# A decoder trunk: the first norm's shift and scale rows on TensorE, and layer 0's last mixer rows loaded with the gate weights

## The chip, the cores and the metric

The kernel runs on one core of a Trainium2 chip. A core has TensorE (matmuls, fp32 here), VectorE, ScalarE, GpSimd (POOL) and SyncE (SP), each with its own instruction stream; they meet only through semaphores. SP's stream issues nearly all weight DMAs. The metric is the device time of one execution in microseconds (us); lower is better.

## The reference, cut to what matters

Two layers run over 256 tokens of 1024 channels. Each has a SwiGLU FFN, a token mixer (an RWKV-7 branch beside an mLSTM branch, joined by sigmoid gates) and a second FFN. Before each part the hidden state is normed and modulated by rows that come from a vector `c`:

```
cond = silu(c)                                   # 1024 values
mod  = cond @ ada_w[l] + ada_b[l]                # 9 rows of 1024: sh0 sc0 gt0 sh1 sc1 gt1 sh2 sc2 gt2
h = rms_norm(x, g0) * (1 + sc0) + sh0;  x += 0.5 * (1 + gt0) * swiglu(h)
h = rms_norm(x, g1) * (1 + sc1) + sh1;  x += (1 + gt1) * token_mixer(h)
h = rms_norm(x, g2) * (1 + sc2) + sh2;  x += 0.5 * (1 + gt2) * swiglu(h)
```

`ada_w[l]` is 1024 x 9216, 37.7 MB a layer, and is used once. `sh0` and `sc0` of layer 0 are needed before the first FFN; `sc2` of layer 0 (columns 7168 to 8191, "the third scale rows") only after its mixer.

## The kernel before

**The start.** `c` is turned into a column and `cond` made. The 2048 columns of `sh0` and `sc0` come in four blocks of 512 columns, each in two DMAs of 512 rows (1 MB): block 0 from POOL's queue into `ada_stage`, blocks 1 to 3 from SP's into `ada_first`, in the order block 2, half of the first FFN weights, block 1, block 3. Blocks 2 and 3 are the scales of channels 0 to 511 and 512 to 1023, blocks 0 and 1 the shifts. Block 0 and 1 are summed by VectorE (`ada_sums`: multiply by a column of `cond`, add, eight times; then a 32x32 block transpose and a reduction; then `ada_columns` on TensorE). Block 2, and three quarters of block 3, are row products on TensorE with one column of `cond` as the weights (`ada_row`); ScalarE copies the row, and TensorE turns it into columns (`row_columns`). `half_factors(0)` and `half_factors(1)` make the scale and shift of the channels of each half, the normed tiles `hT` 0 to 3 and 4 to 7 follow, and `first_halves` multiplies the first four tiles before the last four exist.

**The ring.** All other weights pass through a ring of 12 cells of 4 KB a partition. `ring_places` gives each use its cells and names the use that had them before; SP waits in `room` until TensorE has counted that one free (`slot_free`), and TensorE waits with `landed` for a load. SP issues in program order, so a load that waits holds back all that follow.

**The other rows.** 1024 columns at a time, in four units of 1 MB, are brought by POOL's queue and summed by VectorE in places between its FFN work (`ada_at`): six such blocks in the first FFN of layer 0, five in its second.

**The mixer.** Its weights come as ten projection blocks, then eight gate units `ct` = 0 to 7 (1 MB, three cells taken, two filled), then branch and output weights. A gate unit is loaded in eight pieces of 128 KB over three lanes: a lane holds one piece at a time, and the last piece waits for all three. Gate units 0 and 1 are read by VectorE and TensorE early (the pairs `gates 0` and `gates 1`). For units 2 to 7 TensorE has 96 gate steps, numbered 32 to 127, one matmul of 256 columns each, which `GATE_PLACES` spreads as filler over the chain of small dependent products of the RWKV branch: "num" has steps 32 to 36, "n" 37 to 44, "a" 45 to 52, "b" 53 to 60, "c" 61 to 68, and so on. Unit `ct` begins at step 16 `ct`, with a wait for its load; so unit 3 begins at step 48, the fourth step of place "a". Unit 3 is loaded into the cells of unit 0, unit 4 into those of unit 1, unit 5 into those of unit 2, unit 6 into those of unit 3.

Every matmul of 128 rows and columns in fp32 shows as two records in the trace, a transpose by `turn` as one.

## Time and profile before

| | us |
|---|---|
| median of 3 runs | 1403.44 (1399.76 to 1404.1) |
| the profiled execution's own time | 1401.57 |
| its span, first to last instruction | 1399.8 |
| TensorE busy in the span | 1380.5 (99%) |
| VectorE busy | 1035.5 (74%) |
| ScalarE busy | 299.8 (21%) |
| mean granted TensorE clock | 0.998 |

Times in the rows count from the span's start, 1.8 us less in all than the time of the execution. PE is TensorE, PEld its weight loads, DVE VectorE, ACT ScalarE. A row's bracket gives the idle time before it and what ended that. An execution varies by some 0.3%.

### The profile page before, as it was taken

Reading aid. Unit: us, or ns where it says so; the run is one execution under the profiler, and the core shown is the slowest. Engines: PE = TensorE matmul, PEld = TensorE weight load, DVE = VectorE, ACT = ScalarE, POOL = GpSimd, SP = SyncE. Lnnn points to the kernel's source line nnn. Section 1 sums busy time; section 2 is a strip of 40 time slices with the busy share of each in tenths; the row PEclk is TensorE's granted clock in tenths of the full one; section 3 lists DMA queues with packets and bytes.
Section 4 is the critical chain, followed back from the end, with each engine's and each line's share of the span. In section 5 each row is a group of like instructions: output and inputs, shape, how many; then the busy total and the mean of one; then the engine's idle time right before and its main releaser. Section 6 shows DMA issues by size and latency. Waiting matters only on the chain.

```text
span 1399.8 us, 30879 instructions
## 1 busy us (share of the span) xinstructions
PE 1380.5 (99%) x13632; PEld 1304.0 (93%) x13632; DVE 1035.5 (74%) x1738; ACT 299.8 (21%) x580; POOL 68.4 (5%) x137
## 2 busy tenths in 40 slices
PE   7999999999999999999999999999999999999998
PEld 3999999889988999999999999988898889999998
DVE  5899889778723769987888886887883365856565
ACT  3111101452322031110031110034432302211101
POOL 5010000000000000100000000000000000000000
PEclk9999999999999999999999999999999999999999
DMA  9999785443433758887767886544434257456530
GB/s 347 329 339 324 284 313 174 140 141 104 115 75 122 240 183 276 280 298 292 244 217 248 274 283 241 174 126 143 146 96 105 72 198 241 154 184 205 202 129 31
DMA packets 218085, 283.14 MB, mean 202 GB/s; under 512 B 15272, under 2 KB 183584, under 8 KB 217952
## 3 DMA queue, kind: packets, MB, share of 16 engines
q1 hardware_dynamic: 199008, 211.12, 47.1%
q0 software_dynamic: 17952, 69.21, 14.0%
q8 instruction: 107, 1.75, 0.5%
q10 hardware_dynamic: 992, 0.85, 0.2%
q14 instruction: 26, 0.21, 0.0%
HBM read 280.10 MB, written 1.05 MB: 201 GB/s over the span
## 4 chain that ended last, share of the span: by engine, by line
PE 97%; SPq 1%; DMA 1%; issue 0%; DVE 0%; ACT 0%; ACTq 0%; DVEq 0%
PE ps L1870 96%; DMA arena<-in_ada_w_dram 1%; PE ps L1874 1%; SPq L559 0%; SPq L554 0%; PE ps L2367 0%; DVE hT L1855 0%; DVE x L1257 0%; ACT xn L718 0%; ACTq L254 0%; SPq L552 0%; SPq L551 0%; DVEq L1854 0%; ACTq L1060 0%
## 5 line engine op out<-in xcount | busy, mean ns | idle before, releaser
L1870 PE MATMUL ps<-hT,ring 128*128 128x128 f32 (+2 forms) x2384 | 373.4, 313 | 1.3 <-ACT hT L718 1.3
L1870 PEld LDWEIGHTS ps<-hT,ring 128*128 128x128 f32 (+1 forms) x2384 | 333.7, 191 | 32.3 <-issue 8.3
L1870 PE MATMUL ps<-y_both,arena 128*128 128x128 f32 x2304 | 266.6, 275 | 1.0 <-issue 1.0
L1870 PEld LDWEIGHTS ps<-y_both,arena 128*128 128x128 f32 x2304 | 261.8, 192 | 1.5 <-issue 1.5
L1870 PE MATMUL ps<-arena 32*32 32x32 f32 (+6 forms) x4368 | 203.5, 230 | 3.0 <-issue 3.0
L1870 PEld LDWEIGHTS ps<-arena 32*32 32x32 f32 (+3 forms) x4368 | 192.6, 138 | 12.1 <-issue 10.6
L1870 PE MATMUL ps<-arena,ring 128*128 128x128 f32 (+1 forms) x1344 | 190.8, 294 | 0.0
L1870 PEld LDWEIGHTS ps<-arena,ring 128*128 128x128 f32 x1344 | 175.2, 192 | 6.6
L1084 DVE SCALAR_TENSOR_TENSOR ada_acc<-ada_stage,cond,ada_acc 128x1024 f32<-128x1024 f32 (+1 forms) x119 | 149.0, 1252 | 5.5 <-DMA ada_stage<-in_ada_w_dram 1.5
L1870 PE MATMUL ps<-y_both,ring 128*128 128x128 f32 (+1 forms) x1024 | 150.8, 301 | 0.0
L1870 PEld LDWEIGHTS ps<-y_both,ring 128*128 128x128 f32 x1024 | 138.7, 192 | 6.5
L711 POOL DMA_DIRECT2D ada_stage<-in_ada_w_dram x64 | 45.7, 714 | 901.4 <-DVE ada_acc L1084 637.5
L1870 PE MATMUL ps<-hT,arena 128*128 128x128 f32 x640 | 78.0, 275 | 0.0
L1870 PEld LDWEIGHTS ps<-hT,arena 128*128 128x128 f32 x640 | 74.7, 192 | 0.0
L1313 DVE TENSOR_TENSOR arena<-ring 128x512 f32<-128x512 f32 x44 | 30.3, 690 | 47.1 <-PE ps L1870 46.9
L718 ACT ACTIVATE xn<-ps 128x128 f32<-128x128 f32 (+2 forms) x22 | 7.9, 358 | 267.6 <-PE ps L1870 267.6
L1187 DVE TENSOR_TENSOR raw<-raw,ps 128x256 f32<-128x256 f32 x40 | 16.8, 420 | 61.1 <-ACT raw L782 60.9
L774 ACT ACTIVATE raw<-ps 128x256 f32<-128x256 f32 x40 | 15.4, 386 | 189.9 <-PE ps L1870 189.9
L718 ACT ACTIVATE arena<-ps 128x512 f32<-128x512 f32 (+4 forms) x66 | 34.0, 537 | 93.6 <-PE ps L1870 83.0
L1298 DVE TENSOR_TENSOR arena<-ring 128x1024 f32<-128x1024 f32 x40 | 48.8, 1219 | 4.2 <-DMA ring<-in_ffn_w_in_dram 4.2
L1304 DVE TENSOR_TENSOR arena<-ring,arena 128x1024 f32<-128x1024 f32 x40 | 49.0, 1225 | 1.4
L1302 DVE TENSOR_TENSOR arena<-arena,ring 128x1024 f32<-128x1024 f32 x40 | 48.7, 1218 | 0.0
(316 smaller groups left out, 1389.5 us busy)
## 6 DMA issues: line engine op xcount, KB each, us to landing
ring<-in_ffn_w_in_dram SPq DMA_DIRECT2D x86, 1024.0 KB, 7.7
ada_stage<-in_ada_w_dram POOLq DMA_DIRECT2D x66, 1024.0 KB, 5.9
ring<-in_ffn_w_out_dram SPq DMA_DIRECT2D x44, 1024.0 KB, 6.8
ring<-in_mix_w_in_dram SPq DMA_DIRECT2D x128, 128.0 KB, 2.3
ring<-in_mix_w_in_dram SPq DMA_DIRECT2D x12, 1024.0 KB, 6.0
ring<-in_mix_w_in_dram SPq DMA_DIRECT2D x6, 1536.0 KB, 6.5
ring<-in_mix_w_out_dram SPq DMA_DIRECT2D x8, 1024.0 KB, 5.0
ring<-in_mix_w_in_dram SPq DMA_DIRECT2D x14, 512.0 KB, 6.6
```

What stands on the lines that cost most here:

```text
L711: po.dma_start(wide_stage(v), unit_rows(layer, col, h)).then_inc(ada_full[v % 2], 16)
L718: nc.scalar.activation(out_, in_, func, **kw).then_inc(*AC.step(label))
L774: nc.scalar.activation(part[:, 0, :], ps[:, bank_x, 0:256], ACT.Copy).then_inc(x_copied, 1)
L1084: V.scalar_tensor_tensor(dst, stage[:, k, :], cond[:, k0 + k:k0 + k + 1], dst, ALU.mult, ALU.add).then_inc(ada_done, 1)
L1187: free(V.tensor_tensor(part[:, 0, :], part[:, 0, :], ps[:, bank_w, 0:256], ALU.add))
L1298: V.tensor_tensor(s1, a21, a22, ALU.add).then_inc(w_summed, 1)
L1302: V.tensor_tensor(s2, s1, a11, ALU.subtract).then_inc(w_summed, 1)
L1304: V.tensor_tensor(s4, a12, s2, ALU.subtract).then_inc(w_summed, 1)
L1313: V.tensor_tensor(s1, a21, a22, ALU.add).then_inc(w_summed, 1)
L1870: return nc.tensor.matmul(out_, lhsT, rhs, start=start, stop=stop, **kw)
L1874: return nc.tensor.transpose(out_, in_, ident[0:n, 0:n])
```

## The change

First, the start. All four blocks of layer 0's first shift and scale become products on TensorE. `cond_wide` holds each column of `cond` followed by 31 zeros, so the weights of such a product are 128x32; the four row tiles of a DMA go to four separate quarters of the output partitions (0, 32, 64, 96), and the block's two DMAs add up in place (`rows_of`). The 128x512 result holds partial sums in four rows and zeros in the others. It is copied out whole (by VectorE for blocks 0 and 1, by ScalarE for 2 and 3), turned by four 128x128 transposes (`rows_turned`), and a small VectorE reduction over the four partial sums gives the columns. VectorE's `ada_sums` of the start are gone. `unread` adds two and three products that nobody reads.

Second, the third scale rows of layer 0 are no longer one of the six blocks of its first FFN (five remain). Rows 128 `ct` to 128 `ct` + 127 of them, 0.5 MB, are loaded into the third, so far empty, cell of gate unit `ct`, as two pieces ahead of the unit's eight. VectorE takes them up one unit at a time at eight places of its RWKV chain (`late(0)` to `late(7)`), turns the sum after the head norm, and TensorE and VectorE finish the columns after "merge 3". Since a gate unit's cells now hold something that VectorE reads, `room` has one more wait: a use that takes the cells of gate unit `ct` waits for `late(ct)`.

```diff
+def late_rows_before(use):
+    cells = lambda u: set(range(RING[u][0], RING[u][0] + CELLS[u]))
+    return [ct for ct in range(KT) if U_GATES + ct < use < NC + N_MIX and cells(U_GATES + ct) & cells(use)]
...
+                if l == 0 and late_rows_before(use):
+                    sp.wait_ge(*DV.at(0, f"late {late_rows_before(use)[-1]}"))
...
-                    lane = n % LANES
-                    if n >= LANES:
+                    lane = min(range(LANES), key=lambda m: in_lane[m])
+                    if in_lane[lane]:
                         sp.wait_ge(lane_full[lane], 16 * in_lane[lane])
...
                     room(l, use)
+                    for n in range(LATE_PIECES if l == 0 else 0):
+                        part = slice(n * 512, n * 512 + 512)
+                        piece(n, use, late_rows(l, ct)[:, part],
+                              ada_w[0, ct * P:ct * P + P, LATE_COL + n * 512:LATE_COL + n * 512 + 512])
                     for n in range(PIECES):
...
+            def rows_of(bank, half, stage):
+                for j in range(4):
+                    last = mm(ps[32 * j:32 * j + 32, bank, :], cond_wide[:, 4 * half + j, :], stage[:, j, :],
+                              start=(half == 0), stop=(half == 1))
+                return last
+            def rows_turned(n, bank):
                 for i in range(4):
+                    last = turn(quad(bank)[:, i, :], ada_rows[:, n, i * P:i * P + P])
                 return last
...
+                    dv.wait_ge(*landed(l, U_GATES + ct))
+                    if ct:
+                        dv.wait_ge(*DV.at(l, f"late {ct - 1}"))
+                        free(V.scalar_tensor_tensor(wide, late_rows(l, ct), cond[:, ct:ct + 1], wide,
+                                                    ALU.mult, ALU.add), f"late {ct}")
+                    else:
+                        free(V.tensor_scalar(wide, late_rows(l, ct), cond[:, 0:1], None, ALU.mult), f"late {ct}")
...
                 masked(o32, "o32", 1)
+                late(0)
+                late(1)
                 dv.wait_ge(*AC.at(l, "p2"))
                 flipped("p2t", pt, px[:, 0])
                 power("px 4")
+                late(2)
                 power("px 8")
                 grow("x 8", px[:, 1])
...
                 flipped("x16", xt, px[:, 1])
+                late(3)
                 masked_mk(0)
...
                 for r in range(4):
                     rows, at = slice(32 * r, 32 * r + 32), 32 * (r % 2)
                     free(V.tensor_copy(xf[rows, :, at:at + 32], xt[rows, :, :]))
+                late(4)
                 masked_mk(1)
...
+                if l == 0:
+                    dv.wait_ge(*PE.at(l, "ada late"))
+                    link(l, V.tensor_tensor(mod[:, 56:64], ps[:, 7, 0:8], par_a[:, R_ADA + 56:R_ADA + 64], ALU.add))
```

TensorE at the start, before: the row products have one weight column, and what follows block 2 is its columns (`ada_red,spread` and `ident,xn`) and the first half of the first FFN products (`hT,ring`).

```order
L1870 MATMUL ps<-arena,cond 1x512 [waits first_full2,act_done]
L1870 MATMUL ps<-arena,cond 1x512 x3
L1870 MATMUL ps<-arena,cond 1x512 [waits first_full3]
L1870 MATMUL ps<-arena,cond 1x512 x3
L1874 MATMUL ps<-ident,rows_a 128x96 [waits params_full]
L1870 MATMUL ps<-ada_red,spread 32x4 [waits dve_done]
L1870 MATMUL ps<-ada_red,spread 32x4 x3
L1870 MATMUL ps<-ident,xn 128x1 [waits act_done]
L1870 MATMUL ps<-ident,xn 128x1 x3
L1870 MATMUL ps<-hT,ring 128x256 [waits act_done,half_full]
```

The same place now (`cond_wide` is the padded `cond`, `arena` holds `ada_first`, `xn` the copied rows):

```order
L1917 MATMUL ps<-ada_stage,cond_wide 32x512 x3
L1917 MATMUL ps<-arena,cond_wide 32x512 [waits first_full2]
L1917 MATMUL ps<-arena,cond_wide 32x512 x3
L1917 MATMUL ps<-arena,cond_wide 32x512 [waits first_full3]
L1917 MATMUL ps<-arena,cond_wide 32x512 x3
L1921 MATMUL ps<-ident,rows_a 128x96 [waits params_full]
L1921 MATMUL ps<-ident,xn 128x128 [waits dve_done]
L1921 MATMUL ps<-ident,xn 128x128 x3
L1921 MATMUL ps<-ident,xn 128x128 [waits act_done]
L1921 MATMUL ps<-ident,xn 128x128 x3
L1917 MATMUL ps<-ones 128x256 x2
L1917 MATMUL ps<-hT,ring 128x256 [waits act_done,half_full]
```

Eight row products of block 2 became eight of block 0 and eight of block 2, each 32 output rows wide; the small column products became eight full transposes.

SP's queue at gate unit 3 of layer 0, before: the last piece of unit 2, then unit 3 with its one wait for the ring.

```order
L577 DMA ring<-in_mix_w_in_dram 128x2x128 [waits lane_full2,lane_full1,lane_full0]
L582 DMA ring<-in_mix_w_in_dram 128x2x128 [waits slot_free]
L582 DMA ring<-in_mix_w_in_dram 128x2x128 x2
L582 DMA ring<-in_mix_w_in_dram 128x2x128 [waits lane_full0]
L582 DMA ring<-in_mix_w_in_dram 128x2x128 [waits lane_full1]
L582 DMA ring<-in_mix_w_in_dram 128x2x128 [waits lane_full2]
L582 DMA ring<-in_mix_w_in_dram 128x2x128 [waits lane_full0]
L577 DMA ring<-in_mix_w_in_dram 128x2x128 [waits lane_full2,lane_full1,lane_full0]
```

The same unit now (`ada_w` are the third scale rows):

```order
L595 DMA ring<-in_mix_w_in_dram 128x2x128 [waits lane_full2,lane_full1,lane_full0]
L600 DMA ring<-in_ada_w_dram 128x512 [waits lane_full0,dve_done,slot_free]
L600 DMA ring<-in_ada_w_dram 128x512 [waits lane_full1]
L600 DMA ring<-in_mix_w_in_dram 128x2x128 [waits lane_full2]
L600 DMA ring<-in_mix_w_in_dram 128x2x128 [waits lane_full0]
L600 DMA ring<-in_mix_w_in_dram 128x2x128 [waits lane_full1]
L600 DMA ring<-in_mix_w_in_dram 128x2x128 [waits lane_full2]
L600 DMA ring<-in_mix_w_in_dram 128x2x128 [waits lane_full0]
L600 DMA ring<-in_mix_w_in_dram 128x2x128 [waits lane_full1]
L600 DMA ring<-in_mix_w_in_dram 128x2x128 [waits lane_full2]
L595 DMA ring<-in_mix_w_in_dram 128x2x128 [waits lane_full2,lane_full1,lane_full0]
```

The unit has ten pieces, and its first one waits for VectorE (`dve_done`) too.

VectorE in layer 0's RWKV chain, before, from the first mask to the first power:

```order
L1684 TENSOR_TENSOR arena<-ps,mask_n 128x2x8x32 [waits pe_done,dve_done]
L1693 STREAM_TRANSPOSE arena<-arena 128x512 [waits dve_done]
L1721 TENSOR_TENSOR arena<-arena,spread 128x512
L1684 TENSOR_TENSOR arena<-ps,mask_n 128x2x8x32
L1693 STREAM_TRANSPOSE arena<-arena 128x512 [waits act_done]
L1705 TENSOR_TENSOR arena<-arena,ps 128x256 [waits pe_done]
```

And now:

```order
L1700 TENSOR_TENSOR arena<-ps,mask_n 128x2x8x32 [waits pe_done,dve_done]
L1709 STREAM_TRANSPOSE arena<-arena 128x512 [waits dve_done]
L1750 TENSOR_TENSOR arena<-arena,spread 128x512
L1700 TENSOR_TENSOR arena<-ps,mask_n 128x2x8x32
L1737 TENSOR_SCALAR ada_acc<-ring,cond 128x1024 [waits slot_full0]
L1734 SCALAR_TENSOR_TENSOR ada_acc<-ring,cond,ada_acc 128x1024 [waits dve_done,slot_full1]
L1709 STREAM_TRANSPOSE arena<-arena 128x512 [waits act_done]
L1721 TENSOR_TENSOR arena<-arena,ps 128x256 [waits pe_done]
```

`late(0)` and `late(1)` (L1737, L1734) stand behind the second mask, and `late(0)` is what SP waits for ahead of gate unit 3.

## Rows read from the trace of the kernel before

**Rows 1.** The page: busy time by engine; the chain that ended last, by engine.
```profile
PE 1380.5 (99%) x13632; PEld 1304.0 (93%) x13632; DVE 1035.5 (74%) x1738; ACT 299.8 (21%) x580; POOL 68.4 (5%) x137
...
PE 97%; SPq 1%; DMA 1%; issue 0%; DVE 0%; ACT 0%; ACTq 0%; DVEq 0%
```

**Rows 2.** Windows: stretch, us, busy of PE, PEld, DVE, ACT, POOL, clock, DMA.
```profile
0.00:50.00 50.00, 40.56 (x200) 26.77 (x201) 30.29 (x50) 14.51 (x24) 22.10 (x71) 1.00 1.01 353
50.00:330.00 280.00, 279.99 (x2236) 267.47 (x2235) 249.19 (x406) 65.10 (x130) 15.70 (x22) 1.00 0.72 242
330.00:400.00 70.00, 70.00 (x1210) 64.75 (x1208) 44.69 (x100) 20.58 (x35) 1.04 (x2) 1.00 0.43 105
400.00:450.00 50.00, 47.59 (x1074) 41.05 (x1071) 20.18 (x32) 14.67 (x24) 0.00 (x0) 1.00 0.28 80
```

**Rows 3.** Timeline of PE at the start: start, duration, line, operation, records, idle before.
```profile
6.47 3.50 PE L1874 MATMUL ps<-ident,xn 128*128 128x128 f32 x16 [2.36 <-POOL spread L631]
...
14.98 7.03 PE L1870 MATMUL ps<-arena,cond 128*1 128x512 f32 x16
...
25.05 3.75 PE L1870 MATMUL ps<-hT,ring 128*128 128x256 f32 x16 [1.33 <-ACT hT L718]
29.06 5.31 PE L1870 MATMUL ps<-arena,cond 128*1 128x512 f32 x12 [0.26 <-DMA arena<-in_ada_w_dram]
34.30 1.99 PE L1870 MATMUL ps<-hT,ring 128*128 128x256 f32 x8
...
37.55 12.47 PE L1870 MATMUL ps<-hT,ring 128*128 128x256 f32 x72
```

**Rows 4.** Timeline of ACT, DVE and POOL at the start.
```profile
34.41 0.59 ACT L718 ACTIVATE xn<-ps 1x512 f32<-1x512 f32 x1 [8.51 <-PE ps L1870]
...
38.03 0.16 DVE L1384 SCALAR_TENSOR_TENSOR scale_c<-scale_c,par_a 128x4 f32<-128x4 f32 x1
38.22 1.09 ACT L718 ACTIVATE hT<-hT,shift_c,scale_c 128x256 f32<-128x256 f32 x2 [3.23 <-DVE scale_c L1384]
...
42.20 1.47 POOL L711 DMA_DIRECT2D ada_stage<-in_ada_w_dram  x2 [15.74 <-DMA ring<-in_ffn_w_in_dram]
```

**Rows 5.** Timeline of SP's queue: issues of gate units 2 and 3.
```profile
356.82 4.72 SPq L582 DMA_DIRECT2D ring<-in_mix_w_in_dram  x7
363.51 0.37 SPq L577 DMA_DIRECT2D ring<-in_mix_w_in_dram  x1
363.93 5.88 SPq L582 DMA_DIRECT2D ring<-in_mix_w_in_dram  x7
371.56 0.37 SPq L577 DMA_DIRECT2D ring<-in_mix_w_in_dram  x1
```

**Rows 6.** DMA issues of 360 to 400 us: size, median us to landing.
```profile
ring<-in_mix_w_in_dram SPq DMA_DIRECT2D x35, 128.0 KB, 2.3
```

**Rows 7.** Timeline of DVE in layer 0's RWKV chain.
```profile
375.55 0.68 DVE L1684 TENSOR_TENSOR arena<-ps,mask_n 128x512 f32<-128x512 f32 x1
379.12 0.71 DVE L1693 STREAM_TRANSPOSE arena<-arena 128x512 f32<-128x512 f32 x1 [2.88 <-ACT arena L718]
...
427.65 0.69 DVE L1757 TENSOR_TENSOR arena<-ps,arena 128x512 f32<-128x512 f32 x1 [1.83 <-PE ps L1870]
```

**Rows 8.** DVE's first 1024-column row product, and the group of the others (mean ns).
```profile
53.97 0.75 DVE L1081 TENSOR_SCALAR ada_acc<-ada_stage,cond 128x1024 f32<-128x1024 f32 x1
...
L1084 DVE SCALAR_TENSOR_TENSOR ada_acc<-ada_stage,cond,ada_acc 128x1024 f32<-128x1024 f32 (+1 forms) x119 | 149.0, 1252 | 5.5 <-DMA ada_stage<-in_ada_w_dram 1.5
```

**Rows 9.** Timeline of PE in layer 0's mixer: transposes, gate places "n", "a", 64x64 products.
```profile
371.07 1.04 PE L1874 MATMUL ps<-ident,xn 128*128 128x128 f32 x8
...
373.44 3.72 PE L1870 MATMUL ps<-hT,ring 128*128 128x256 f32 x16
...
378.31 3.72 PE L1870 MATMUL ps<-hT,ring 128*128 128x256 f32 x16
...
413.42 1.10 PE L1870 MATMUL ps<-ring 64*64 64x128 f32 x32
```

**Rows 10.** Windows, the last 4 us, where PE has stopped (clock 0.56).
```profile
1395.00:1399.00 4.00, 0.04 (x1) 0.00 (x0) 0.98 (x2) 1.18 (x2) 0.00 (x0) 0.56 0.70 262
```

More of the change, by code:

```diff
@@ L162, in ada_blocks @@
     if half == 0:
-        return [(l, 2 * D + n * WIDE_BLOCK) for n in range(2 if l else 0, 6)]
+        return [(l, 2 * D + n * WIDE_BLOCK) for n in range(2, 6) if l] or \
+            [(l, 2 * D + n * WIDE_BLOCK) for n in range(5)]
     return [(l, 8 * D)] + [(l + 1, n * WIDE_BLOCK) for n in range(4) if l + 1 < DEPTH]
@@ L830, in _ @@
             for n in range(2):
-                ac.wait_ge(*PE.at(None, f"row {n}"))
-                act(xn[0:1, n, 0:BLOCK], ps[0:1, n, :], ACT.Copy, f"row {n}")
+                ac.wait_ge(*PE.at(None, f"rows {2 + n}"))
+                act(ada_rows[:, 2 + n, :], ps[:, 1 - n, :], ACT.Copy, f"rows {2 + n}")
                 ac.wait_ge(*DV.at(None, f"factors {n}"))
@@ L1378, in half_factors @@
             def half_factors(n):
+                for row, bank in ((n, 3), (2 + n, 2 - n)):
+                    free(V.tensor_reduce(first_cols[:, 4 * row:4 * row + 4], quad(bank)[:, :, 0:P:32], AXX, ALU.add))
+                dv.wait_ge(*DV.last())
                 some, scales = slice(4 * n, 4 * n + 4), slice(8 + 4 * n, 12 + 4 * n)
-                free(V.tensor_tensor(shift_c[:, some], ps[:, 3, some], par_a[:, R_ADA + 4 * n:R_ADA + 4 * n + 4], ALU.add))
-                link(None, V.tensor_tensor(scale_c[:, some], ps[:, 3, scales],
+                free(V.tensor_tensor(shift_c[:, some], first_cols[:, some], par_a[:, R_ADA + 4 * n:R_ADA + 4 * n + 4], ALU.add))
+                link(None, V.tensor_tensor(scale_c[:, some], first_cols[:, scales],
                                            par_a[:, R_ADA + 8 + 4 * n:R_ADA + 12 + 4 * n], ALU.add))
@@ L1426, in _ @@
-            free(V.tensor_reduce(ada_red[:, 3, :], view(ada_turn[:, :], 16, 32), AXX, ALU.add), "ada 3")
+            free(V.memset(cond_wide[:, :, :], 0.0), "cond room")
+            dv.wait_ge(*PE.at(None, "first rows 1"))
+            free(V.tensor_copy(ada_rows[:, 0, :], ps[:, 0, :]), "rows 0")
+            dv.wait_ge(*AC.at(None, "rs start"))
+            for k in range(2):
+                free(V.tensor_tensor(hT[:, k, :], x[:, k, :], rs[:, :], ALU.mult), f"normed start {k}")
+            first_normed(1)
@@ L1427, in _ @@
+            params(None, "params next", 7)
+            dv.wait_ge(*PE.at(None, "half"))
+            half_factors(0)
+            first_tiles((3,))
+            for b in (2, 3):
+                first_normed(b)
+            dv.wait_ge(*PE.at(None, "rows 1"))
+            free(V.tensor_copy(ada_rows[:, 1, :], ps[:, 2, :]), "rows 1")
             link(None, V.memset(stat[:, :, :], 0.0))
@@ L1758, in _ @@
                                      by_chunk(diag), ALU.add), "gt")
+                late(7)
                 dv.wait_ge(*PE.at(l, "qt"))
@@ L1778, in _ @@
                 head_scaled(l, y_heads, 16, 64, "r")
+                if l == 0:
+                    for h in range(2):
+                        dv.wait_ge(*DV.last(l))
+                        link(l, V.transpose(ada_turn[:, :], ada_acc[:, h, :]))
+                        link(l, V.tensor_reduce(ada_red[:, h, :], view(ada_turn[:, :], 16, 32), AXX, ALU.add),
+                             "late columns" if h else None)
                 for p in range(4):
@@ L2082, in first_halves @@
                            stop=False, skip_group_check=True)
-            pe.wait_ge(*AC.at(None, "cond"))
+            pe.wait_ge(*AC.at(None, "cond wide"))
             pe.wait_ge(*AC.at(None, "x 1 1"))
-            ada_row(0, 0, KT).then_inc(*PE.step("row 0"))
+            for u in range(2):
+                pe.wait_ge(ada_full[u], 16)
+                last = rows_of(0, u, ada_stage[:, u])
+                last.then_inc(*PE.step(f"first rows {u}"))
+            for u in range(2):
+                pe.wait_ge(first_full[2 + u], 16)
+                last = rows_of(1, u, ada_first[:, 2 + u])
+            last.then_inc(*PE.step("rows 2"))
             pe.wait_ge(params_full, 16 * 2)
             params("params next", 7, rest=False)
-            pe.wait_ge(*DV.at(None, "ada 0"))
-            ada_columns(3, 0, 0, 1, "ada 0")
-            row_columns(0, 8).then_inc(*PE.step("half"))
+            pe.wait_ge(*DV.at(None, "rows 0"))
+            rows_turned(0, 3)
+            pe.wait_ge(*AC.at(None, "rows 2"))
+            rows_turned(2, 2).then_inc(*PE.step("half"))
+            unread(2)
             pe.wait_ge(half_full, 32)
             first_halves(0)
-            ada_row(1, 0, ROW_TILES).then_inc(*PE.step("row 1"))
-            first_halves(1, (0,))
-            pe.wait_ge(*DV.at(None, "ada 1"))
-            ada_columns(3, 4, 1, 1, "ada 1")
-            row_columns(1, 12)
-            pe.wait_ge(*DV.at(None, "ada 3"))
-            ada_columns(3, 12, 3, 1, "ada", start=False)
-            first_halves(1, (1,))
+            pe.wait_ge(*DV.at(None, "factors 0"))
+            for u in range(2):
+                pe.wait_ge(first_full[u], 16)
+                last = rows_of(2, u, ada_first[:, u])
+            last.then_inc(*PE.step("rows 1"))
+            first_halves(1)
+            for u in range(2):
+                pe.wait_ge(first_full[4 + u], 16)
+                last = rows_of(0, u, ada_first[:, 4 + u])
+            last.then_inc(*PE.step("rows 3"))
+            pe.wait_ge(*DV.at(None, "rows 1"))
+            rows_turned(1, 3)
+            pe.wait_ge(*AC.at(None, "rows 3"))
+            rows_turned(3, 1).then_inc(*PE.step("ada"))
+            unread(3)
             for l in range(DEPTH):
@@ L2625, in _ @@
                 pe.wait_ge(*DV.at(l, "merge 3"))
+                if l == 0:
+                    pe.wait_ge(*DV.at(l, "late columns"))
+                    ada_columns(7, 0, 0, 2, "ada late")
                 for p in range(3):
```

74 lines of the change are left out of this document (28 added, 46 removed).

## The prediction

> **What bounds the kernel now.** I read the busy shares and the chain of waits first [rows 1]: TensorE is busy for 99% of the span and 97% of the chain is its own work. So an engine beside it costs time only where it makes TensorE wait, and work taken off VectorE gains nothing by itself. The windows by stage say where TensorE waits at all [rows 2]: 9.4 of the first 50 us, nothing from 50 to 400, 2.4 us from 400 to 450 (the RWKV chain). The change touches three of these stages. I read the start and the mixer in the timelines, engine by engine, and then SP's queue, since a new wait stands in it.
>
> **The start.** Its end is the moment from which TensorE runs without a gap on FFN products of the last four `hT` tiles. Before, 72 records begin at 37.55; the first 8 of them (0.21 us each, as 16 took 3.72 [rows 9], so 1.7 us) are the rest of `first_halves`, so the new tiles are taken up at 39.3. The last 1 MB of block 3 is needed in the row product that begins at 29.06 and goes on with its second DMA after four of its six products [rows 3], each two records of 5.31/12 = 0.44 us: 29.06 + 4 x 0.88 = 32.6. Weights are fetched a product ahead, so I put that landing at 32.0. It stays: the same bytes in the same order.
>
> Now step by step. What does a `rows_of` of four products cost? Each product streams 512 columns in 0.88 us. One after the other they take 3.5 us; if all four quarters of the array work side by side, 0.9. The nearest row is the 64x64 products, which also share row groups and differ in output quarter: 32 records of 128 columns took 1.10 us [rows 9], where 16 records of 256 columns one after the other took 3.72, so 32 of 128 would take 3.7. They run 3.4 deep. By that a group costs 3.5/3.4 = 1.0 us; I take 1.0 with bounds of 0.9 and 3.5.
> - The sum of squares ends at 15.0 (that is where the next row begins [rows 3]). Four groups follow, the last one's data used by 18.4 before as well: end at 19.3. Copy 0.6, eight transposes: 0.13 each as 8 took 1.04 [rows 9], reduction, three small VectorE steps of 0.16 [rows 4]: `hT` 0 is ready at about 23, where before TensorE took it up at 25.05 [rows 3].
> - First products of 3.75 us to 26.8; two groups to 28.8; eight products of `first_halves(1)`, 3.7 us, to 32.5; two groups to 34.5.
> - ScalarE's copy 0.6 [rows 4] and its handover, to 35.2; four transposes 0.5, to 35.8; from there before took from 37.6 to 38.8 for the factors and the first tile [rows 4], and now two more small reductions add 0.4: tiles 4 and on from 37.4.
>
> That is 39.3 - 37.4 = 1.9 us sooner. Less some pacing by ScalarE's two tiles (1.09 us for two, against 0.43 a product), which were hidden behind `first_halves` before: **-1.8 us**, bounds -2.5 (groups at 0.9, no pacing) and -0.6 (groups at 1.3). The FFN weights behind it don't undo it: pair 1 has landed when POOL is released at 42.20 [rows 4], and is needed 16 products of 0.43 after 37.4, at 44.3.
>
> On this the Trainium skill ("TensorEngine Tiling (Array Packing)", Tiling Modes) lists 128x32 as four independent tiles, which agrees with the 3.4 of the 64x64 row; the same page says that a change of tiling mode drains TensorE. By the first, a group would cost 0.9 and the start gain about 2.4 us; the sum goes by the row.
>
> **The first FFN.** VectorE loses four units: eight products of 1.25 [rows 8], two transposes and reductions. TensorE has no gap there [rows 2], so this is worth 0, and 4 MB less on the queues too.
>
> **The chain: eight row products on VectorE.** 0.75 us for the first and 1.25 for each of the other seven [rows 8], 9.5 us. All stand in idle stretches of VectorE, which is busy for 20 of the 50 us from 400 on [rows 2]: `late(0)` and `late(1)`, 2.0 us, into the 2.88 us ahead of 379.12; `late(6)`, 1.25, into the 1.83 ahead of 427.65, the shortest [rows 7]. Cost 0 if the data is there. The finishing of the columns (4 x 0.7 on VectorE before the turned heads come, 4 tiny products on TensorE that are taken from an earlier call) 0 to 0.3; I take 0.
>
> **The wait in SP's queue.** This is the term that decides. Before, gate unit 3 was issued from 363.93, right after unit 2, and its last piece at 371.56 [rows 5]; with 2.3 us to landing [rows 6] it was there at 374. TensorE needs it at step 48. Place "a" begins with step 45 at 378.31 and a step takes 3.72/8 = 0.46 us [rows 9], so step 48 is due at 379.7: 6 us of reserve. Now the unit's first piece waits for `late(0)`, since unit 3 takes unit 0's cells. VectorE comes to `late(0)` when the second mask ends, 375.55 + 0.68 = 376.2 [rows 7], and ends it at 377.0. From there the whole unit has to be loaded: before, the last of eight pieces was issued 7.6 us after the first (6.7 for unit 2) [rows 5]. Nine pieces ahead of the last are three rounds over three lanes, as seven were, but the third round is now full and two pieces are of 256 KB: I add 0.7 and take 8.3, with bounds of 7.0 and 10. Landing 2.5 later: 377.1 + 8.3 + 2.5 = 387.9. TensorE stands from 379.7 to 387.9: **+8.2 us**, bounds 6.5 and 10.
>
> Nothing hides this: TensorE's queue is in order, and behind step 48 are five more steps of "a", the first power, and through it all of ScalarE's and VectorE's chain. Its gaps at 400 to 450 [rows 2] are made by that chain and stay. It happens once: unit 4 follows at 385.5 and is there at 396, while step 64 (fourth of place "c") moves to about 400; units 5 to 7 wait for `late(2)` to `late(4)`, which then have over 6 us of reserve each. Units 1 and 2 are ten pieces too: unit 2, issued from 356.82 [rows 5], lands at 367.6, before step 32 in place "num", which stands ahead of the transposes of 371.07 [rows 9], with about 1 us to spare. Layer 1 has no such wait.
>
> **The clock after the stall.** In the last four microseconds TensorE has stopped and the granted clock is 0.56 of 2.4 GHz [rows 10]: it has gone to the lower level (1.2 GHz) within about a microsecond. After its idle start TensorE's first 16 transposes took 0.22 us each [rows 3], later ones 0.13 [rows 9]: 16 x 0.09 = 1.4 us lost. I take the same 1.4 here (bounds 0 and 2): **+1.4 us**. The Trainium skill ("TensorE: Matmul & The Clock Gate", Part 1) says the clock falls to half while TensorE idles and comes back after sustained work; the trace's last row agrees, and by it the sum would be the same.
>
> **Sum.** -1.8 + 8.2 + 1.4 = +7.8 us. Against its own time the profiled execution would go from 1401.57 to 1409.4; that execution was 1.9 us under the median of 1403.44, so the median goes to about **1411**.
>
> **Rivals.**
> - *The stall is hidden.* If unit 3 were there by step 48, only the start's gain would be left: 1403.44 - 1.8 = 1401.6, faster by 0.1%, or 1400.9 at the bound. It decides at 379.7: the load must take 2.6 us after `late(0)`, about the 2.3 of one piece, or `late(0)` must come some 8 us sooner. Against it: VectorE's masks wait for TensorE's products, not for VectorE. For it: only the chance that I misread which unit's cells are meant. With a start that gains more than I think (over 4.2 us) it would be faster by over 0.3%.
> - *The quarters don't work side by side.* Then 32 products of 0.88 us stand instead of eight groups of 1.0: 20 us more, with no wait of the start long enough to hide them, and 1411 + 20 = 1431. For it: no product of 128 rows by 32 columns and 512 streamed stands in the trace. Against it: the 64x64 row.
> - *The load is slower or a second unit stalls.* If a lane's round takes 3.3 us with 256 KB pieces, unit 3 lands at 390, and unit 2 misses step 32 by a microsecond: 1403.4 - 1.8 + 10 + 1 + 2 = 1415.
> - *A short stall.* If pieces of the emptier queue land in 1.5 us, the unit takes 6.5: stall 4.3, clock 1: 1407.
>
> **How the numbers follow.** Forecast (stall of 6.5 to 10) 0.68; short stall 0.10; slower load 0.10; serial quarters 0.05; hidden 0.07. Bounds of the likeliest: -2.5 + 6.5 + 0 = +4 and -0.6 + 10 + 2 = +11.4, so 1407.4 to 1414.8. The range over the cases, with the spread of a median of runs, is 1405 to 1417. A change of 0.3%, 4.2 us, is what measurement can tell from none. Faster by more than that: 0.04. Within it: the rest of the hidden case and most of the short stall, 0.13. Slower: 0.83.
>
> **What would show it.** A gap of TensorE of 6 to 10 us in the middle of place "a", some 379 us in, ended by the DMA of gate unit 3, with SP's queue waiting for VectorE just before; a lower granted clock in the few us behind it; TensorE taking up `hT` 4 to 7 at about 37; no VectorE products at the start, and four quarter products within about 1 us. It would be wrong if unit 3's first piece is issued before `late(0)`, if TensorE has no gap there, or if groups of four take 3 us.

## The result and the profile after

Four executions of the changed kernel took 1411.0 us (1410.06 to 1411.88), four of the kernel before on the same chip 1402.65 (1399.76 to 1404.1): a ratio of 1.0066, with an interval of 1.0054 to 1.0078. The forecast was about 1411. The profiled execution took 1410.06 us, its span is 1408.3 (1399.8 before), and its mean granted clock 0.995 (0.998 before).

TensorE's timeline of the kernel after, from the mixer's place "num" on (columns as in [rows 3]):

```profile
367.04 2.43 PE L1917 MATMUL ps<-hT,ring 128*128 128x256 f32 x10
...
371.67 3.72 PE L1917 MATMUL ps<-hT,ring 128*128 128x256 f32 x16
...
376.54 1.56 PE L1917 MATMUL ps<-hT,ring 128*128 128x256 f32 x6
387.22 4.00 PE L1917 MATMUL ps<-hT,ring 128*128 128x256 f32 x10 [9.12 <-DMA ring<-in_mix_w_in_dram]
```

The ten records at 367.04 are place "num", the 16 at 371.67 place "n". Place "a" is the 16 records that begin at 378.31 in [rows 9]. Now it is cut after six: three steps of gate unit 2, then 9.12 us of nothing, then five steps of unit 3. The same unit in SP's queue (lines 600 and 595 issue it), which answers to [rows 5]:

```profile
354.83 0.82 SPq L600 DMA_DIRECT2D ring<-in_ada_w_dram  x2
355.70 5.85 SPq L600 DMA_DIRECT2D ring<-in_mix_w_in_dram  x7
364.83 0.37 SPq L595 DMA_DIRECT2D ring<-in_mix_w_in_dram  x1
375.18 0.82 SPq L600 DMA_DIRECT2D ring<-in_ada_w_dram  x2
376.05 7.04 SPq L600 DMA_DIRECT2D ring<-in_mix_w_in_dram  x7
385.04 0.37 SPq L595 DMA_DIRECT2D ring<-in_mix_w_in_dram  x1
```

Unit 2's last piece is issued at 364.83 and unit 3's first at 375.18; before, the two followed each other without a pause. What it waits for is in VectorE's timeline, of which [rows 7] is the part before:

```profile
373.78 0.68 DVE L1700 TENSOR_TENSOR arena<-ps,mask_n 128x512 f32<-128x512 f32 x1
374.38 0.74 DVE L1737 TENSOR_SCALAR ada_acc<-ring,cond 128x1024 f32<-128x1024 f32 x1
375.22 1.28 DVE L1734 SCALAR_TENSOR_TENSOR ada_acc<-ring,cond,ada_acc 128x1024 f32<-128x1024 f32 x1
```

`late(0)` is line 1737: it ends at 375.12, and SP issues 0.06 us later. So the ten us of SP's pause are the place of that one instruction in VectorE's program. The windows around the gap (columns as in [rows 2]; the clock stands ahead of the DMA share):

```profile
375.00:380.00 5.00, 3.10 (x136) 2.23 (x134) 2.12 (x3) 1.68 (x3) 0.00 (x0) 1.00 0.56 159
380.00:385.00 5.00, 0.00 (x0) 0.00 (x0) 0.00 (x0) 0.00 (x0) 0.00 (x0) 0.52 0.52 132
385.00:390.00 5.00, 2.78 (x7) 2.22 (x8) 0.00 (x0) 0.00 (x0) 0.00 (x0) 0.50 0.64 181
390.00:395.00 5.00, 5.00 (x155) 4.26 (x154) 1.80 (x5) 1.70 (x4) 0.00 (x0) 0.96 0.56 136
```

All four compute engines stand still from 380 to 385, and the DMA queues move only 132 GB/s, where the start moves 353 [rows 2]: it is not bandwidth that holds the load. The clock has fallen to its lower level (1.2 of 2.4 GHz), and stays there while TensorE already works again.

TensorE at the start, the rows that answer to [rows 3]:

```profile
11.47 5.43 PE L1917 MATMUL ps<-hT,ones 128*128 128x256 f32 x16 [1.35 <-ACT hT L743]
16.84 1.92 PE L1917 MATMUL ps<-ada_stage,cond_wide 128*32 128x512 f32 x16
18.58 1.90 PE L1917 MATMUL ps<-arena,cond_wide 128*32 128x512 f32 x16
...
23.48 3.75 PE L1917 MATMUL ps<-hT,ring 128*128 128x256 f32 x16 [0.77 <-ACT hT L743]
27.16 1.92 PE L1917 MATMUL ps<-arena,cond_wide 128*32 128x512 f32 x16
29.02 3.72 PE L1917 MATMUL ps<-hT,ring 128*128 128x256 f32 x16
32.67 1.92 PE L1917 MATMUL ps<-arena,cond_wide 128*32 128x512 f32 x16
34.52 1.44 PE L1921 MATMUL ps<-ident,xn 128*128 128x128 f32 x8
...
37.57 10.72 PE L1917 MATMUL ps<-hT,ring 128*128 128x256 f32 x64 [0.31 <-ACT hT L743]
```

Two groups of four products are 16 records in 1.92 us, 0.96 a group. The new tiles are taken up at 37.57; before, 72 records began at 37.55, whose first eight were old work, so that is 1.74 us sooner (12.47 less 10.72 is 1.75 for those eight).

### The profile page after: what moved, and what is told of

It is laid out like the page before. It is cut to its first block, busy times and chain, and to the rows that moved or that the text cites. A ratio compares the mean times of both kernels' runs of the same rounds, so it can differ in the third digit from the quotient of the medians.

```text
span 1408.3 us, 30962 instructions
## 1 busy us (share of the span) xinstructions
PE 1381.3 (98%) x13662; PEld 1306.8 (93%) x13662; DVE 1021.1 (73%) x1722; ACT 300.3 (21%) x581; POOL 61.9 (4%) x133
## 3 DMA queue, kind: packets, MB, share of 16 engines
q8 instruction: 107, 1.75, 0.5%
## 4 chain that ended last, share of the span: by engine, by line
PE 97%; DVE 1%; DMA 1%; issue 1%; ACT 0%; POOL 0%; SPq 0%; ACTq 0%; POOLq 0%; DVEq 0%
PE ps L1917 95%; PE ps L1921 1%; DMA ring<-in_mix_w_in_dram 0%; DVE x L1284 0%; DMA ring<-in_ada_w_dram 0%; PE ps L2430 0%; DVE hT L1902 0%; ACT xn L743 0%; ACT hT L743 0%; POOL ada_stage L657 0%; DVE arena L1700 0%; POOL spread L653 0%; DVE arena L1709 0%; SPq L600 0%; DVE xn L1276 0%
## 5 line engine op out<-in xcount | busy, mean ns | idle before, releaser
L1917 PE MATMUL ps<-hT,ring 128*128 128x128 f32 (+2 forms) x2384 | 375.4, 314 | 10.2 <-DMA ring<-in_mix_w_in_dram 9.1
L1111 DVE SCALAR_TENSOR_TENSOR ada_acc<-ada_stage,cond,ada_acc 128x1024 f32<-128x1024 f32 x105 | 134.6, 1282 | 3.2
L736 POOL DMA_DIRECT2D ada_stage<-in_ada_w_dram x60 | 42.8, 714 | 913.6 <-DVE ada_acc L1111 644.3
L743 ACT ACTIVATE xn<-ps 128x128 f32<-128x128 f32 (+1 forms) x22 | 7.9, 359 | 266.0 <-PE ps L1917 265.7
L1325 DVE TENSOR_TENSOR arena<-ring 128x1024 f32<-128x1024 f32 x40 | 48.7, 1218 | 6.3 <-DMA ring<-in_ffn_w_in_dram 6.2
L1326 DVE TENSOR_TENSOR arena<-ring 128x1024 f32<-128x1024 f32 x40 | 48.7, 1217 | 0.0
```

What stands on the lines that cost most here:

```text
L736: po.dma_start(wide_stage(v), unit_rows(layer, col, h)).then_inc(ada_full[v % 2], 16)
L743: nc.scalar.activation(out_, in_, func, **kw).then_inc(*AC.step(label))
L1111: V.scalar_tensor_tensor(dst, stage[:, k, :], cond[:, k0 + k:k0 + k + 1], dst, ALU.mult, ALU.add).then_inc(ada_done, 1)
L1325: V.tensor_tensor(s1, a21, a22, ALU.add).then_inc(w_summed, 1)
L1326: V.tensor_tensor(s3, a11, a21, ALU.subtract).then_inc(w_summed, 1)
L1917: return nc.tensor.matmul(out_, lhsT, rhs, start=start, stop=stop, **kw)
```

## The experiments

Each kernel is told by its edit against the kernel after, where nothing else is said; medians stand beside those of before on the same chip, with the ratio and its 95% interval. The ratio is not the quotient of the two medians: it differs from that by up to 0.001, or 1.4 us, so a microsecond between two medians proves nothing.

**`late(0)` ahead of the masks.** It stands behind the last operation of the gate pairs now (`late` itself is defined there), so only its place changes.

```diff
                 pair_sums("gates 1")
+                late(0)
...
                 masked(o32, "o32", 1)
-                late(0)
                 late(1)
```

> The changed kernel with one product moved: late(0) stands behind the sums for the pair gates 1 (about 356 us in the changed kernel's time) and no longer behind the second mask (374.4). My theory (the wait of gate unit 3's load for late(0) makes the 9.1 us gap and the slow clock behind it): unit 3 is issued right behind unit 2's last piece (364.8), its last piece at about 374.7, landed at 377, and TensorE needs it at 378.1, so the gap goes or stays under 1 us: 1400.5 us, between 1399 and 1402.5. Rival 1 (the added 0.5 MB in each gate unit is what costs): the loads are as long as before, a gap stays, over 1405. Rival 2 (VectorE's eight products delay the chain): nothing changes, 1411.

1402.62 us against 1402.07: 1.0008 (0.9999 to 1.0017). The change's loss of 8.4 us has shrunk to 0.6. Place "a" has no gap of 9 us any more; what is left of waits for gate units are two small ones, at steps 64 and 80, which are units 4 and 5 (the expectation of the four-lane kernel calls them 5 and 6):

```profile
390.67 2.43 PE L1918 MATMUL ps<-hT,ring 128*128 128x256 f32 x10 [0.41 <-DMA ring<-in_mix_w_in_dram]
...
402.59 2.43 PE L1918 MATMUL ps<-hT,ring 128*128 128x256 f32 x10 [0.55 <-DMA ring<-in_mix_w_in_dram]
```

and its queue shows unit 4:

```profile
376.12 0.88 SPq L600 DMA_DIRECT2D ring<-in_ada_w_dram  x2
377.05 8.21 SPq L600 DMA_DIRECT2D ring<-in_mix_w_in_dram  x7
388.45 0.37 SPq L595 DMA_DIRECT2D ring<-in_mix_w_in_dram  x1
```

Unit 4 takes 12.3 us from its first issue to its last here (unit 3 took 10.2), and the two waits say that this is a little slower than TensorE comes to use it. So the wait was nearly all of the loss. The median is 0.1 us over the range I gave and 2.1 over my value. The two gaps (0.96 us) and a slow start (the new tiles are taken up at 37.94) don't explain that: the profiled execution has both and took 1400.72. What lifts the others isn't shown.

**The same place, without the ada pieces.** The third scale rows of layer 0 are left out: they aren't loaded, and VectorE reads gate weights in their place, so the wait stays and the bytes go.

```diff
-            return slot(l, U_GATES + ct)[:, 2048:3072]
+            return slot(l, U_GATES + ct)[:, 0:1024]
...
-                    for n in range(LATE_PIECES if l == 0 else 0):
+                    for n in range(0):
```

> The changed kernel without the sixteen pieces of third scale rows; the eight products on VectorE read the unit's first 1024 gate weights in their place (so the third scale rows of layer 0 are left out), and the wait for late(0) to late(7) stays. It parts the wait from the bytes. Theory: unit 3 still starts at 375.2 but takes 7.6 us to its last piece and 2.3 to land, 385.1, so the gap is 7.0 us and not 9.1: about 1409 us (1408 to 1410). Rival 1 (the bytes): no gap is left, 1401.

1408.55 us against 1402.07: 1.0054 (1.0041 to 1.0066).

```profile
383.62 4.64 PE L1917 MATMUL ps<-hT,ring 128*128 128x256 f32 x10 [6.75 <-DMA ring<-in_mix_w_in_dram]
```

```profile
373.96 5.45 SPq L600 DMA_DIRECT2D ring<-in_mix_w_in_dram  x7
381.40 0.37 SPq L595 DMA_DIRECT2D ring<-in_mix_w_in_dram  x1
```

Eight pieces from first to last issue take 7.4 us, ten took 9.9. So 6.75 of the 9.12 us are the wait itself and 2.4 are the two 256 KB pieces: a hit for the theory, against the rival that the bytes alone make the gap.

**The changed kernel with four lanes instead of three.**

```diff
-PIECES, LANES, PACED_BRANCH = 8, 3, 2
+PIECES, LANES, PACED_BRANCH = 8, 4, 2
```

> The changed kernel with four lanes, late(0) left where the change put it. Theory (the wait for late(0) makes the gap; lanes only set how long a unit's load is): unit 3 starts at 375, and as the four-lane run's loads took 7.9 us to the last piece when the queue was else idle, the gap is about 7 us: 1408.5 us (1407 to 1410). Rival (the lanes were what counted in the four-lane run): 1400.

1410.27 us against 1402.1: 1.005 (1.0037 to 1.0063), 0.3 us above the range I gave.

```profile
385.77 4.63 PE L1917 MATMUL ps<-hT,ring 128*128 128x256 f32 x10 [7.84 <-DMA ring<-in_mix_w_in_dram]
```

The load is 8.6 us instead of 9.9 and the gap 1.3 shorter. But the ten records behind it take 4.63 us, where they took 4.00, which gives half of that back (the kernel without the ada pieces shows the same, 4.64). A faster queue can't hide a load that is started too late.

**TensorE kept busy through the gap.** 19 products of `ones` whose result nobody reads stand ahead of the wait for unit 3, to keep the clock up.

```diff
+                            if l == 0 and ct == 3:
+                                pe.wait_ge(*DV.at(l, "num read"))
+                                for _ in range(19):
+                                    mm(ps[:, GATE_BANK[ct], 0:T], ones[:, 0:P], ones[:, 0:T])
```

> The changed kernel with 19 products of 256 columns that nobody reads, put on TensorE just ahead of its wait for gate unit 3 (19 x 0.43 = 8.1 us, inside the 9.1 us gap). Theory: the load still ends the wait at the same moment, but the granted clock stays at 1.00 and the ten records behind the gap take 2.3 us, not 4.0: 1411.0 - 1.8 = 1409.2 us. Rival (the slow records are slow for the data's sake and not by the clock): 1411.

```profile
378.31 8.37 PE L1917 MATMUL ps<-ones 128*128 128x256 f32 x38
...
387.44 2.43 PE L1917 MATMUL ps<-hT,ring 128*128 128x256 f32 x10 [0.77 <-DMA ring<-in_mix_w_in_dram]
389.80 1.99 PE L1917 MATMUL ps<-arena 32*32 32x64 f32 x128
```

The ten records take 2.43 us where they took 4.00, so the slow clock's price behind the gap is 1.57 us, and the next power begins at 389.80, where it began at 391.15. But the time is 1410.8 against 1402.07, 1.0066 (1.0052 to 1.008): the ratio is that of the kernel after, and my 1409.2 was missed. In the profiled execution place "num" had waited 0.28 us for unit 2, so that `late(0)` came 0.4 us later and the load's end 0.2; a later wait for a gate unit cost 0.53 us, and TensorE's idle time put down to "issue" was 4.2 us in sum, against 3.1 in the kernel after. The local price is shown; that it is worth as much in the total isn't.

**All row products into one quarter of the output.** The first shift and scale aren't computed rightly, since the four row tiles add up in rows 0 to 31.

```diff
-                    last = mm(ps[32 * j:32 * j + 32, bank, :], cond_wide[:, 4 * half + j, :], stage[:, j, :],
-                              start=(half == 0), stop=(half == 1))
+                    last = mm(ps[0:32, bank, :], cond_wide[:, 4 * half + j, :], stage[:, j, :],
+                              start=(half == j == 0), stop=(half == 1 and j == 3))
```

> The changed kernel with all eight row products of a block written to the same quarter of the output partitions (0 to 31) in one sum, so that no two can work side by side; the columns that follow from the three other quarters are leftovers, so the first shift and scale are not computed rightly. Theory (four quarters work side by side, 0.96 us a group of four): a group takes 4 x 0.88 = 3.5 us; eight groups are 20 us longer, and the time is 1411 + 20 = 1431 (1427 to 1433). Rival (the row products were fast for another reason, say few weight columns): 0.96 us a group as before, 1411.

```profile
16.73 7.05 PE L1917 MATMUL ps<-ada_stage,cond_wide 128*32 128x512 f32 x16
23.63 7.03 PE L1917 MATMUL ps<-arena,cond_wide 128*32 128x512 f32 x16
```

7.05 us against 1.92 for the same eight products: in four quarters they run 3.7 deep. From start to start, which leaves out the tail of the last one, it is 6.90 (16.73 to 23.63) against 1.74 (16.84 to 18.58), 4.0 deep. The kernel took 1433.28 us against 1402.68, 1.0219 (1.02 to 1.0238), 22 us more than the changed one. That was the rival "the quarters don't work side by side", priced at 1431; the time is 0.3 us over the range above, 1427 to 1433.

**The start alone.** The second half of the change is undone: six blocks in the first FFN again, and no third rows in the gate units.

```diff
-        return [(l, 2 * D + n * WIDE_BLOCK) for n in range(2, 6) if l] or \
-            [(l, 2 * D + n * WIDE_BLOCK) for n in range(5)]
+        return [(l, 2 * D + n * WIDE_BLOCK) for n in range(2 if l else 0, 6)]
...
-                    for n in range(LATE_PIECES if l == 0 else 0):
+                    for n in range(0):
...
-                    first, end = (32, 64) if l else (16, 56)
+                    first, end = (32, 64) if l else (16, 64)
```

> Only the start of the change; the third scale rows are again the sixth block of layer 0's first FFN, and gate units and mixer are as before the change. Theory: the start alone is worth what the trace showed, TensorE takes up the FFN 1.7 to 1.8 us sooner and keeps that to the end: 1400.9 us, between 1399.5 and 1402. Rival (the start's gain is given back in the first FFN, whose weights land at the same time as before): 1402.6, no change.

1399.87 us against 1402.07, 0.9994 (0.9982 to 1.0006), with executions from 1399.06 to 1405.67. The interval holds both my 1400.9 and the rival's "no change". The profile shows more: the start is gained, and lost in the first FFN:

```profile
47.33 5.52 PE L1913 MATMUL ps<-y_both,arena 128*128 128x128 f32 x48
...
164.95 2.05 PE L1913 MATMUL ps<-y_both,arena 128*128 128x128 f32 x16 [1.32 <-ACT raw L800]
...
231.51 2.95 PE L1913 MATMUL ps<-arena 128*128 128x128 f32 x24 [1.34 <-DVE arena L1340]
```

The first row begins 2.53 us sooner than in the kernel before (49.86), and the two gaps take 2.66 us back: place "n" begins at 373.96, 0.5 us later than in [rows 9] (0.4 of it I didn't trace). Ahead of each gap VectorE has waited for a unit of the six blocks, 2.91 us where the kernel before has no wait and 1.89 where it has 0.42, and the sums, transposes and reductions behind it are in front of the work that TensorE needs:

```profile
157.30 2.61 DVE L1108 SCALAR_TENSOR_TENSOR ada_acc<-ada_stage,cond,ada_acc 128x1024 f32<-128x1024 f32 x2 [2.91 <-DMA ada_stage<-in_ada_w_dram]
...
223.99 2.60 DVE L1108 SCALAR_TENSOR_TENSOR ada_acc<-ada_stage,cond,ada_acc 128x1024 f32<-128x1024 f32 x2 [1.89 <-DMA ada_stage<-in_ada_w_dram]
```

So it is the landing of these units as much as VectorE's sums that TensorE comes too early for; that is near the rival above, with the units of the six blocks in place of the FFN's own weights. Five blocks have fewer of both, and no run parts the two. With the same edit and four lanes:

> The start of the change alone (six blocks in the first FFN, no rows in the gate units) with four lanes. Theory (the start's gain is given back in the first FFN when VectorE has six blocks of sums there; lanes play no part): as the run with the start alone, 1400.5 (1399.5 to 1402), at least 1 us over the four-lane run of both parts with late(0) early (1398.7). Rival (the start alone carries the gain): 1398.7.

1402.34 us against 1402.1, 0.9999 (0.9987 to 1.0011), and the same two gaps, 2.75 us at 167.01 and 1.34 at 235.34. That is a hit against the rival's 1398.7, 0.3 us over the range.

**The mixer's part alone**, with the old start, `late(0)` early and four lanes. The diff of the start is taken back, in short:

```diff
-                    ada_sums(wide, wide_stage(v), 0, 2, 2 * (n % UNITS), 2 * v)
+                    ada_sums(wide, wide_stage(v), 0, 2, 2 * (n % UNITS), 16 + 2 * v)
...
-                free(V.tensor_reduce(first_cols[:, 4 * row:4 * row + 4], quad(bank)[:, :, 0:P:32], AXX, ALU.add))
```

> The start of the kernel before, with the change's mixer part (third scale rows in the gate units, five blocks in the first FFN), late(0) early and four lanes. The start alone won 2.5 us by 47 us and had lost them at 373 us, by two waits of 1.3 us in the first FFN for VectorE's sums; with five blocks there (the changed kernel) no such wait came. Theory (the two parts need each other: fewer sums on VectorE are what lets the start's gain through, and are worth nothing alone): 1402.1, the time of the kernel before, within 0.8 us. Rival (the lighter first FFN is worth something by itself): 1400.5 or less.

1402.18 us against 1402.68, 0.9999 (0.999 to 1.0009): nothing, as expected. TensorE has no gap from 50 to 400 us in it, and none was there to be filled before.

**Both parts, `late(0)` early, four lanes** (the two edits shown above together), then the same with five lanes, then with four and `late(1)` early as well:

```diff
                 pair_sums("gates 1")
+                late(0)
+                late(1)
```

> The changed kernel with late(0) behind the sums for gates 1 (as in the run before) and with four lanes for the paced pieces instead of three. The run with late(0) early left two gaps of 0.4 and 0.55 us on the DMAs of gate units 5 and 6, with a unit taking 11 to 12 us from its first piece to the next unit's. Theory (what is left of the loss is the length of a unit's load, ten pieces in three lanes): a unit takes about 8.5 us, both gaps go, and the median falls by 1 us or more to 1400.0 (1399 to 1401.5). Rival (the unit's length costs nothing, the rest is scatter of the runs): same as with late(0) early, 1402.6.

> As the run with four lanes, with five. Theory: nothing waits for a gate unit's load any more, so no further gain: within 0.5 us of the run with four lanes. Rival (more pieces in flight disturb TensorE's own reads): slower by 1 us or more.

> Four lanes, and late(1) early as well as late(0). In the four-lane run with late(0) early, gate unit 4's first piece still waited for late(1) from 370.7 to 374.8 and TensorE waited 1.17 us for unit 5. Theory: unit 4 starts 4 us sooner, unit 5 too, that gap goes, but VectorE is 1.3 us later with the parts of the pairs gates 0 and 1, which TensorE's product n needs: between 0 and -1 us against the four-lane run, 1398.3. Rival (the chain ahead of n has no reserve on VectorE): +1 us, 1399.8.

| | us | before | ratio |
|---|---|---|---|
| four lanes | 1398.68 | 1402.68 | 0.9978 (0.9969 to 0.9987) |
| five lanes | 1399.87 | 1402.68 | 0.9982 (0.9973 to 0.9991) |
| four lanes, `late(1)` early | 1399.97 | 1402.1 | 0.9978 (0.9969 to 0.9987) |

All three beat the kernel before, by 2 to 4 us between the medians, and the changed one by 11 or more. None came where I put it: four lanes is 0.3 us under its range, and the other two are 1.2 and 1.3 us over the first where I had "within 0.5" and "0 to -1". That is the size of both rivals, but the intervals of the ratios overlap, so neither is decided.

In the first, unit 3 is issued at once behind unit 2 and complete in its queue at 370.32, unit 4 waits 4 us for `late(1)` (VectorE, 373.43 to 374.70), and TensorE has one gap, at step 80, for unit 5:

```profile
361.98 0.37 SPq L595 DMA_DIRECT2D ring<-in_mix_w_in_dram  x1
362.47 0.91 SPq L600 DMA_DIRECT2D ring<-in_ada_w_dram  x2
363.42 4.53 SPq L600 DMA_DIRECT2D ring<-in_mix_w_in_dram  x7
370.32 0.37 SPq L595 DMA_DIRECT2D ring<-in_mix_w_in_dram  x1
374.77 0.82 SPq L600 DMA_DIRECT2D ring<-in_ada_w_dram  x2
```

```profile
400.86 2.43 PE L1918 MATMUL ps<-hT,ring 128*128 128x256 f32 x10 [1.17 <-DMA ring<-in_mix_w_in_dram]
```

The third takes that wait away too (TensorE is 70.00 of 70 us busy from 330 to 400, and has no gap at step 80), and its median is no better. But the wait for `late(1)` isn't enough to make the gap: with five lanes unit 4 waits for it as well (its first piece is issued at 374.92, unit 3's last at 369.91) and step 80 has no gap. In the first kernel the last piece of unit 5 is issued at 396.39 and TensorE goes on 4.5 us later; behind the last piece of unit 3 in the kernel after it was 2.2. I had expected 8.5 us a unit with four lanes; unit 3 takes 7.9, but unit 5 of the same kernel 11.5 (384.92 to 396.39), so the lanes alone don't set it, and what does isn't settled.

One thing is left unexplained here. The first of these kernels differs from `late(0)` early with three lanes by the lanes alone, and its ratio is 0.9978 against 1.0008, intervals apart, some 4 us. The two profiled executions don't show it: their spans are 1398.5 and 1398.7, and their waits for gate units 1.17 and 0.96 us.

**The kernel before with four lanes**, to see whether they are the gain by themselves:

> The kernel before with four lanes and nothing else. Theory: TensorE waits for no gate unit there, so the time stays: 1402.6, within 1 us. Rival (the lanes alone are worth the gain of the four-lane run): 1399.

1401.15 us against 1402.1, 0.9991 (0.9981 to 1.0001): no gain beyond the interval, 0.45 us under what I allowed, and far from the rival's 1399. Its profiled execution shows something else:

```profile
25.19 6.72 PE L1870 MATMUL ps<-hT,ring 128*128 128x256 f32 x16 [1.31 <-ACT hT L718]
```

These are the records of 3.75 us in [rows 3], at little more than half the speed; the granted clock from 10 to 50 us was 0.91 here. What stands there doesn't depend on the lanes: the start's speed differs between executions.

## Why the prediction was right, step by step

**The start: -1.8 forecast, -1.74 measured.** The steps came at 23.5, 27.2, 29.0, 32.7, 34.5 and 37.57, where I had 23, 26.8, 28.8, 32.5, 34.5 and 37.4. One group was 0.96 us (1.0), not the 3.5 of the far bound. The value is right by two errors that cancel. The sum of squares took 5.43 us in this execution and 3.72 before, so the first group begins at 16.84 and not at 15.0; and the groups and the steps behind them up to `hT` 0 were shorter than written, 3.6 and 3.0 us for 4.3 and 3.7. (A small slip beside it: 16 records in 3.72 us are 0.23 each, not 0.21.) With the new start the sum of squares took 3.72 us in five of the experiments' profiles; at that speed the start gains more. But not the whole 1.7 us, for something else becomes late next, as the kernel with `late(0)` early and four lanes shows:

```profile
32.79 1.06 PE L1918 MATMUL ps<-arena,cond_wide 128*32 128x512 f32 x8 [0.51 <-DMA arena<-in_ada_w_dram]
...
36.84 10.72 PE L1918 MATMUL ps<-hT,ring 128*128 128x256 f32 x64 [0.31 <-ACT hT L743]
```

It is the last 1 MB of block 3, whose landing I had put at 32.0. The new tiles are then taken up at 36.84, a gain of 2.5 us, my bound. On the price of a group the Trainium skill ("TensorEngine Tiling (Array Packing)", Tiling Modes) agrees with the trace: four independent tiles by its list, 3.7 deep by the rows, 4.0 from start to start. TensorE's timeline has no idle time where groups and products of 128x128 meet.

**The first FFN: 0, right for the sum, wrong as a reason.** TensorE had no gap there before and has none after:

```profile
50.00:330.00 280.00, 280.00 (x2229) 267.44 (x2228) 239.26 (x398) 65.27 (x130) 12.84 (x18) 1.00 0.69 227
```

But the four units taken off VectorE aren't worth nothing in every company. With the new start and six blocks TensorE idles 2.7 us there. "Work taken off VectorE gains nothing by itself" held only for a start that ends where it did; once TensorE comes 2.5 us sooner, it waits for VectorE, and VectorE for its units. The gaps show that. The medians agree for four lanes, where all four kernels were measured (the mixer's part with `late(0)` early):

| four lanes | six blocks, no late rows | the mixer's part |
|---|---|---|
| old start | 0.9991 (0.9981 to 1.0001) | 0.9999 (0.999 to 1.0009) |
| new start | 0.9999 (0.9987 to 1.0011) | 0.9978 (0.9969 to 0.9987) |

Each part alone gains nothing, both together some 3 us; only the interval of the old start without the mixer's part overlaps the last one, by 0.0006. With three lanes they don't show it: 0.9994 for the start alone and 1.0008 for both with `late(0)` early. So the new start needs the lighter first FFN, but that isn't all that it needs.

**The chain's products: 0, right.** All eight fit into VectorE's idle time. `late(6)`, whose place was the shortest:

```profile
432.56 1.28 DVE L1734 SCALAR_TENSOR_TENSOR ada_acc<-ring,cond,ada_acc 128x1024 f32<-128x1024 f32 x1
434.52 0.69 DVE L1794 TENSOR_TENSOR arena<-ps,arena 128x512 f32<-128x512 f32 x1 [0.68 <-PE ps L1917]
```

0.68 us of VectorE's idle time is left behind it, where 1.83 less 1.25 would be 0.6.

**The wait: +8.2 forecast, +9.12 measured, inside its bounds.** The mechanism is the one I gave, and moving that one instruction takes the loss away. The mis-sized term is the load: 9.9 us from the first piece's issue to the last's (8.3 forecast, bounds 7.0 and 10), with 2.2 to landing (2.5). The pieces of 256 KB cost 2.4 us more than eight pieces alone, not 0.7 more. The dates are all 1.8 us sooner than written there, as the start's gain had arrived by then on both sides; the difference doesn't change. Unit 2 was nearer to a wait than I wrote, with nothing to spare and not a microsecond: its last piece is issued at 364.83, lands some 2.2 us later, and place "num" begins at 367.04. With TensorE kept busy through the gap, where nothing else differs up to there, it waited 0.28 us.

**The clock: +1.4 forecast, +1.6 measured.** 4.00 us for ten records against 2.43 in the kernel that kept TensorE busy; the granted clock was 0.52 and 0.50. But the price isn't one number: behind gaps of 6.75 and 7.84 us the ten records took 4.64 and 4.63 us, 2.2 more. And that my 1.4 came close was luck in its source. I had taken it from 16 transposes of 0.22 us at the start [rows 3], and in that stretch, 6 to 10 us, the granted clock reads 1.00, so those rows don't show what the lower level costs.

**The sum: +7.8 forecast, +8.35 between the medians.** By the terms it is -1.74 + 9.12 + 1.57 = +8.95. The profiled spans differ by 8.5. Part of what lies between is the idle time that the waits put down to "issue": 4.0 us in before, and after (sum, count, longest)

```profile
PE ps L1917 <- issue: 2.5, 5, 0.8
```

with 0.6 more on another line, 0.9 less in all, which would make 8.05; the 0.4 or so that is then missing I didn't trace. That the time is 1411.0 to the tenth is luck: the forecast stood on a median before of 1403.44 from three executions, four gave 1402.65, and the difference was 0.55 us larger than forecast. The largest gap of before stood right behind this place:

```profile
401.79 0.97 PE L1870 MATMUL ps<-arena 64*64 64x128 f32 x25 [1.52 <-issue]
```

**The rivals.** "Hidden", priced at 1401.6, is what the kernel with `late(0)` early makes true, at 1402.62. Serial quarters, priced at 1431, came to 1433.28. The slower load (a stall of 10) came half way with 9.12, and unit 2 didn't stall in the profiled execution, if only just.

## What to carry to other kernels

When free cells of a ring get a second reader, the place of its read in that engine's program decides when the next load starts. Set it by when the cells are needed again, not by where the engine idles: here one VectorE instruction of 0.74 us, put behind two masks that wait for TensorE, made a gap of 9 us of TensorE, of which 2.4 were the added bytes. Count the load that then starts from nothing in rounds of the paced queue, with the new pieces' size.

An engine with no gap is only in time for its present partner: before a zero is written for work taken off it, ask whether another part of the change makes it late.

## What the runs showed that was not expected

- The length of a paced load varies: a gate unit of 1.5 MB takes 7.9 to 11.5 us from first to last issue in one and the same kernel with four lanes, and up to 12.3 with three, while the DMA queues are about half busy (0.52 to 0.64 in the windows above, of the kernel after). Why it varies is open.
- TensorE's first 30 us run at a speed that differs between executions: 16 records in 3.72 or 5.3 to 5.8 us at 11 us, or 3.75 against 6.72 at 25 us. Behind the slow first, the row products begin some 1.7 us later. The granted clock from 10 to 20 us reads 1.00 in the slow profiles as in the fast ones, so it doesn't tell them apart; the cause is open.
- "Issue" gaps of TensorE of up to 1.5 us come and go between executions, 2 to 4 us in sum, and blur every effect of a microsecond that is read from one profile. It took some ten executions of a kernel to tell 3 us from none.
